# Overflow branch moved behind the expert blocks, with the expert results loaded in front of it

## The reference, cut to what matters

```python
# per token: the best of 4 groups, in it the best 2 of 8 experts, gates from two softmaxes
hid = silu(xb @ w_gate[e]) * (xb @ w_up[e])      # 1024 -> 256
y   = hid @ w_down[e]                            # 256 -> 1024
x   = x + segment_sum(y * gate, token)           # two rows for each token
x   = x + (p[i] @ w_ple[i]) * sigmoid(rmsnorm(x, g_ple[i]) @ w_ple_gate[i])
```

## Time and profile before

| | |
|---|---|
| median of 3 runs | 2473.81 us (2472.18 to 2477.26) |
| the profiled execution's own time | 2474.32 us |
| its span | 2472.4 us |
| TensorE busy | 2280.0 us, 92% |
| VectorE, ScalarE, GpSimd busy | 993.5, 588.0, 402.7 us |
| DMA | 402.86 MB, mean 163 GB/s |

### The profile page before, as it was taken

How to read it: one execution, slowest core, us unless ns; L and a number is a source line. 1 busy time by engine, 2 the same in 40 slices (tenths; PEclk the granted TensorE clock), 3 DMA queues, 4 the chain that set the end, 5 groups by cost and what they waited for, 6 DMA issues and landing times. The chain is left out here.

```text
span 2472.4 us, 29130 instructions
## 1 busy us (share of the span) xinstructions
PE 2280.0 (92%) x11792; PEld 1688.7 (68%) x11792; DVE 993.5 (40%) x1701; ACT 588.0 (24%) x1213; POOL 402.7 (16%) x399
## 2 busy tenths in 40 slices
PE   7989999689889989999698979899999999999998
PEld 6666788444447767788554446687767887888887
DVE  5545533311135444643411116455653334322234
ACT  3533301211123342410311113323441002100012
POOL 2011111112211101111111212111101211112111
PEclk9999999799989999999899999899999999999999
DMA  5114436699962202234789994332222333233321
GB/s 159 52 53 107 126 109 250 262 415 421 422 272 77 68 26 71 65 94 146 304 337 422 421 373 148 86 86 71 79 69 73 102 104 97 85 99 98 95 102 69
DMA packets 291897, 402.86 MB, mean 163 GB/s; under 512 B 31534, under 2 KB 230958, under 8 KB 273834
## 3 DMA queue, kind: packets, MB, share of 16 engines
q1 hardware_dynamic: 276000, 372.56, 42.1%
q0 software_dynamic: 10176, 16.81, 1.8%
q10 hardware_dynamic: 5578, 11.51, 1.7%
HBM read 388.98 MB, written 30.15 MB: 170 GB/s over the span
## 5 line engine op out<-in xcount | busy, mean ns | idle before, releaser
L138 PE MATMUL banks<-h_split,w_high 128*128 128x512 f32 x2624 | 825.7, 396 | 2.3 <-PEq L3142 1.7
L138 PEld LDWEIGHTS banks<-h_split,w_high 128*128 128x128 f32 x2624 | 480.9, 188 | 104.3 <-issue 8.2
L190 DVE TENSOR_TENSOR w_low<-w_raw,w_high 128x1024 fp32r<-128x1024 f32 (+1 forms) x264 | 316.8, 1201 | 502.3 <-POOL w_high L179 502.2
L179 POOL CAST w_high<-w_raw 128x1024 fp32r<-128x1024 f32 (+1 forms) x264 | 277.0, 1050 | 1458.9 <-PE banks L138 1334.1
L138 PE MATMUL banks<-h_split,w_low 128*128 128x512 f32 x1312 | 512.1, 390 | 0.0
L138 PEld LDWEIGHTS banks<-h_split,w_low 128*128 128x128 f32 x1312 | 246.2, 188 | 52.3
L138 PE MATMUL banks<-w_high,op_split 128*128 128x512 f32 x736 | 228.5, 390 | 1.4 <-DVE mg_part L1355 1.1
L1950 PE MATMUL banks<-expert_ring,ex_xsT 128*64 128x256 f32 x1472 | 181.6, 403 | 21.6 <-DMA expert_ring<-in_w_exp_up 18.6
L1950 PEld LDWEIGHTS banks<-expert_ring,ex_xsT 128*64 128x64 f32 x1472 | 108.0, 145 | 81.1 <-DMA expert_ring<-in_w_exp_up 20.5
L138 PEld LDWEIGHTS banks<-w_high,op_split 128*128 128x128 f32 x736 | 138.1, 188 | 31.9 <-DVE mg_part L1355 2.4
L138 PE MATMUL banks<-w_low,op_split 128*128 128x512 f32 x368 | 143.2, 389 | 0.0
(11 more groups left out here) (416 smaller groups left out, 2727.8 us busy)
## 6 DMA issues: line engine op xcount, KB each, us to landing
w_raw<-in_w_in SPq DMA_DIRECT2D x142, 512.0 KB, 4.0
expert_ring<-in_w_exp_gate SPq DMA_DIRECT2D x46, 1024.0 KB
expert_ring<-in_w_exp_up SPq DMA_DIRECT2D x46, 1024.0 KB
expert_ring<-in_w_exp_down SPq DMA_DIRECT2D x46, 1024.0 KB, 22.2
w_raw<-in_w_gu SPq DMA_DIRECT2D x44, 512.0 KB, 4.0
region<-in_w_exp_gate SPq DMA_DIRECT2D x20, 1024.0 KB
region<-in_w_exp_up SPq DMA_DIRECT2D x20, 1024.0 KB
region<-in_w_exp_down SPq DMA_DIRECT2D x20, 1024.0 KB, 17.6
```

What stands on the lines that cost most here:

```text
L138: last = nc.tensor.matmul(out, left, right, start=(start and n == 0), stop=(stop and n == 2), skip_group_check=True)
L179: self.nc.gpsimd.tensor_copy(self.high[:, i % self.SPLIT, 0:n], self.raw[:, i % self.RAW, 0:n]).then_inc(self.high_ready, 1)
L190: self.nc.vector.tensor_tensor(self.low[:, i % self.SPLIT, 0:n], self.raw[:, i % self.RAW, 0:n], self.high[:, i % self.SPLIT, 0:n].bitcast ...
```

## The change

The expert blocks are now part of `merge_and_route`, in the same program block as the routing. The block ends only after them, after six of the eight half-tiles of p @ w_ple, the first three splits, and after `results.load` has been issued. Then come the register load and the branch over the overflow blocks; where it is taken, it works through the 16 overflow blocks and loads the results again. The border block begins with GpSimd clearing semaphores, for which every engine waits (`swept`), and goes on with the last two half-tiles, the additions and the rest.

Within the expert blocks: TensorE starts with transposes 0, gate and up 0, hidden 0, gate and up 1, down 0, hidden 1, transposes 1, down 1, and goes on with block 2 as before. A gather's transposes are signalled in two halves, and VectorE and TensorE go on with each half. A gather is issued one pair earlier. SyncE refills the first two slots in the order gate and up 6, gate and up 7, down 6, down 7. The arithmetic for `route_spill_expert` stands behind the first pair. The space in SBUF that is kept for the descriptors of GpSimd's DMAs goes from the default of 16384 to 4096 bytes of each partition.

```diff
@@ merge_and_route
             expert_loads.issue(sp, 10)
+            for part in (e.load_gate_up, e.load_down):
+                for n in (EXPERT_SLOTS, EXPERT_SLOTS + 1):
+                    part(sp, n, n)
+            for n in range(EXPERT_SLOTS + 2, EXPERTS):
+                e.load(sp, n)
+            sp.wait_ge(spill_ready, 1)
+            for n in range(EXPERTS, e.blocks):
+                e.load(sp, n)
+            for q in (e.pairs - 2, e.pairs - 1):
+                c = (q + 1) % GATHERS
+                sp.wait_ge(e.turned, 2 * q + 2)
+                sp.dma_start(*embedding.load_pair(c)).then_inc((p_landed0, p_landed1)[c], 16)
+            sp.wait_ge(e.down_done, e.blocks - 2)
+            gate_stream.loads(sp, 0, gate_stream.RAW)
+            e.stored(sp)
+            results.load(sp)
...
+                nc.gpsimd.memset(e.xs[:, u, :], 0.0).then_inc(cleared, 1)
             pool.wait_ge(cleared, GATHERS)
             pool.wait_ge(norm.stored, 16 * NT)
             pool.wait_ge(token_ready, 2)
-            for q in range(GATHERS):
-                nc.gpsimd.indirect_dma_start(out=xs[:, q, :], out_offset=None, in_=xn_rows[:, :],
-                                             in_offset=bass.IndirectOffsetOnAxis(ap=r.token[:, q:q + 1], axis=0),
-                                             bounds_check=last_token, oob_is_err=False).then_inc(gathered[q], 16)
+            e.gather(pool, 0, last_token)
+            e.gather(pool, 1, last_token)
+            e.pooled(pool, last_token, last_row, row_ready)
+            pool.wait_ge(e.down_done, e.blocks)
+            gate_stream.split_highs(pool, 0, gate_stream.SPLIT)
...
+            pe.wait_ge(p_taken, 1)
+            e.turn(pe, 0)
+            e.gate_up(pe, 0)
+            e.turn_hidden(pe, 0)
+            e.gate_up(pe, 1)
+            e.down(pe, 0)
+            e.turn_hidden(pe, 1)
+            e.turn(pe, 1)
+            pe.wait_ge(row_ready, 1)
+            e.down(pe, 1)
+            e.multiply(pe, 2)
+            pe.wait_ge(p_landed0, 16)
+            pe.wait_ge(p_landed1, 16)
+            for i in range(EARLY_PRODUCTS):
+                wait(pe, embedding.ready, i - 1)
+                embedding.product(i, k.ps[:, i % 2, :]).then_inc(multiplied, 1)
...
+            act.preload_act_table_set("silu_and_others")
+            e.activate(act)
+            for i in range(EARLY_PRODUCTS):
+                act.wait_ge(multiplied, i + 1)
+                embedding.take(i, k.ps[:, i % 2, :])
...
+            e.weigh(dve, 0)
+            e.hidden(dve, 0)
+            e.hidden_turned(dve, 0)
+            e.hidden(dve, 1)
+            e.hidden_turned(dve, 1)
+            e.weigh(dve, 1)
+            link(V.tensor_tensor(ended, ends[:, 1:].unsqueeze(1).to_broadcast([P, SPILL, NE]),
+                                 iota[:, 0:SPILL].unsqueeze(2).to_broadcast([P, SPILL, NE]), ALU.is_le))
+            link(V.tensor_reduce(out=spill_f[:, 0:SPILL], in_=ended.bitcast(F32), axis=AX.X, op=ALU.add))
+            link(V.tensor_scalar(spill_f[:, 0:SPILL], spill_f[:, 0:SPILL], float(NE - 1), None, ALU.min),
+                 V.tensor_copy(spill_f[:, SPILL:SPILL + 1], ends[:, NE:]))
+            V.tensor_copy(r.spill_expert[:], spill_f[0:1, :]).then_inc(spill_ready, 1)
+            e.vectors(dve, 2)
+            for i in range(gate_stream.SPLIT):
+                gate_stream.split_low(dve, i)
...
-SPILL_SLOTS = (5,)
+SPILL_SLOTS = (2,)
 SBUF_END = 229344
-GATHERS = 2
+GATHERS, OUTPUTS = 2, 3
+FIRST_PAIR = 2
+EARLY_PRODUCTS = 6
...
@@ Experts
+    def load_gate_up(self, sp, n, expert):
+        U = len(self.slots)
+        wait(sp, self.gu_done, n - U + 1)
+        for dst, src in expert_parts(self.slots[n % U], *(w[self.layer, expert] for w in self.weights))[0:2]:
+            sp.dma_start(dst, src).then_inc(self.w_landed[n % U], 16)
+
+    def load_down(self, sp, n, expert):
+        U = len(self.slots)
+        wait(sp, self.down_done, n - U + 1)
+        dst, src = expert_parts(self.slots[n % U], *(w[self.layer, expert] for w in self.weights))[2]
+        sp.dma_start(dst, src).then_inc(self.down_landed[n % U], 16)
+
...
+    def gather_next(self, pool, q, last_token):
+        if q < self.pairs:
+            pool.wait_ge(self.turned, 2 * (q - GATHERS + 1))
+            self.gather(pool, q, last_token)
+
...
+    def pooled(self, pool, last_token, last_row, row_ready=None):
+        self.gather_next(pool, GATHERS, last_token)
+        if row_ready:
+            pool.wait_ge(row_ready, 1)
+        for n in range(self.blocks):
+            if n == 1:
+                self.gather_next(pool, GATHERS + 1, last_token)
+            elif n and n % 2 == 0:
+                self.gather_next(pool, n // 2 + GATHERS + 1, last_token)
+            self.scatter(pool, n, last_row)
...
+    def turn(self, pe, q):
+        pe.wait_ge(self.gathered[q % GATHERS], 16 * (q // GATHERS + 1))
+        wait(pe, self.xsT_ready, 2 * q)
+        for c in range(DC):
+            last = self.nc.tensor.transpose(self.k.ps[:, c // 4, (c % 4) * P:(c % 4 + 1) * P], self.xs[:, q % GATHERS, c::DC],
+                                            self.k.ident[:])
+            if c % 4 == 3:
+                last.then_inc(self.turned, 1)
...
+        wait(pe, self.hid_ready, n - 1)
+        for c in range(DC):
+            if c % 4 == 0:
+                pe.wait_ge(self.xsT_ready, 2 * q + 1 + c // 4)
...
+    def multiply(self, pe, start):
+        for n in range(start, self.blocks):
+            self.gate_up(pe, n)
+            if n % 2 == 0 and n // 2 + 1 < self.pairs:
+                self.turn(pe, n // 2 + 1)
+            if n > start:
+                self.down(pe, n - 1)
+            self.turn_hidden(pe, n)
+        self.down(pe, self.blocks - 1)
...
+    def weigh(self, dve, q):
+        wait(dve, self.gu_done, 2 * (q - GATHERS + 1))
+        for b in (0, 1):
+            dve.wait_ge(self.turned, 2 * q + 1 + b)
+            self.nc.vector.tensor_tensor(self.xsT[:, q % GATHERS, 4 * b:4 * b + 4, :],
+                                         self.k.ps[:, b, :].rearrange("p (c n) -> p c n", c=4),
+                                         self.r.gain[:, 4 * b:4 * b + 4].unsqueeze(2).to_broadcast([P, 4, P]),
+                                         ALU.mult).then_inc(self.xsT_ready, 1)
...
@@ spilled_experts
+    xs = k.room(ctx, tag + "_xs", [P, GATHERS, D])
...
+        for n in range(e.blocks):
+            e.load(sp, n)
+        e.stored(sp)
+        for t in range(NT):
+            sp.wait_ge(results.landed[t], 16)
+            sp.dma_start(*results.part(t)).then_inc(reloaded, 16)
+        sp.wait_ge(reloaded, 16 * NT)
...
@@ embed_per_layer
-        pe.wait_ge(embedding.ready, NT)
-        for t in range(NT):
-            embedding.product(NT + t, k.ps[:, t, :]).then_inc(multiplied, 1)
+        for i in range(EARLY_PRODUCTS, 2 * NT):
+            wait(pe, embedding.ready, i - 1)
+            embedding.product(i, k.ps[:, i % 2, :]).then_inc(multiplied, 1)
...
-        for t in range(NT):
-            act.wait_ge(multiplied, t + 1)
-            embedding.take(NT + t, k.ps[:, t, :])
+        for i in range(EARLY_PRODUCTS, 2 * NT):
+            act.wait_ge(multiplied, i - EARLY_PRODUCTS + 1)
+            embedding.take(i, k.ps[:, i % 2, :])
...
@@ border
+    done, swept = sweep
     with k.nc.Block() as block:
         @block.sync
         def _(sp):
-            moe[0](sp)
+            sp.wait_ge(swept, 1)
             ple[0](sp)
             attention[0](sp)
 
         @block.gpsimd
         def _(pool):
-            moe[1](pool)
+            clear(k, pool, done)
+            pool.sem_inc(swept, 1)
             ple[1](pool)
             attention[1](pool)
 
         @block.tensor
         def _(pe):
-            moe[2](pe)
+            pe.wait_ge(swept, 1)
             ple[2](pe)
             attention[2](pe)
...
@@ first_layer
-        ended = k.used_sems - lasting
+                                   gate_stream.low_ready, gate_stream.used, swept]}
+        merge_and_route(k, "rt", st, attention, yb_ready, m, op, r, xn_rows, route_loads, expert_loads, embedding, gate_stream,
+                        results, e, ended)
         ctx.close()
         spilled = nc.values_load(r.spill_expert[0:1, SPILL:SPILL + 1], min_val=0, max_val=SPILL)
         with nc.If(spilled > ALWAYS - EXPERTS), ExitStack() as rest, nc.Block() as block:
-            more = experts(k, rest, rest, "sp", r, i, EXPERTS, SPILL, xn_rows, y_rows, *weights, xs, gathered)
+            more = spilled_experts(k, rest, "sp", tiles, r, i, xn_rows, y_rows, weights, results)
...
@@ kernel
-    nc = bacc.Bacc("TRN2", target_bir_lowering=False, num_devices=1)
+    nc = bacc.Bacc("TRN2", target_bir_lowering=False, num_devices=1, dynamic_dma_scratch_size=4096)
```

(9 more changed lines are left out.)

338 lines of the change are left out of this document (143 added, 195 removed).

## The result

The changed kernel takes 2458.04 us (median of 4 runs, 2457.09 to 2460.14) beside 2473.64 us of the kernel before (median of 4 runs): a ratio of 0.9936, with a 95% interval of 0.9919 to 0.9953. The forecast was 2464.8, with a range from 2460.5. The direction was right; 15.6 us were gained where 9.0 were forecast. So the way is certain, and the size is known only to some 4 us.

What follows compares the result with a forecast made beforehand. The prediction took weight traffic to bound the expert blocks; terms 1 and 2 (-19.4 us) and term 3 (+10.4) gave -9.0 against the profiled 2474.32, hence a median of 2464.8 us, range 2460.5 to 2472.

Steps and rivals of the forecast that it cites:

- What bounds the stage: Expert blocks: time is the weight traffic; savings count only if refills start earlier or run with fewer holes.
- Term 1: Start of the expert blocks: block end and branch leave the path from gather to transposes; first refill 8.6 and 8.2 us earlier.
- Term 2: Expert refills: the new order of SyncE's queue closes a hole behind the first refill, 1.3 us in each layer.
- costed at nothing: Silu table load, gates, overflow arithmetic, SyncE's wait, GpSimd's queue with its gathers, and later loads: priced at 0 us.
- Term 3, the additions: Behind the experts: VectorE's additions wait for a block end after six evictions, 4.7 us later in each layer.
- Term 3, the clock: Behind the experts: TensorE's pause drops its clock, half-tiles and transposes outlast the additions; 0.5 us lost in each layer.
- A: Expert start gives less: clock rises no sooner, hole only moves; 14.0 us gained, tail costs 10.4; 2470.2 us, chance 0.13.
- B: Branch behind the experts: VectorE pays like TensorE and a microsecond more, 4.3 us a layer; 2473.4 us, chance 0.07.
- C: GpSimd's descriptors run out of room, 160 us a layer, about 2785 us; chance 0.05 together with other tail losses.

Runs made afterwards that it cites:

- the dummies: Kernel before plus seven matmuls without use in TensorE's two waits in front of the gate product: 2472.18 us, ratio 0.9999.
- the repeat: The changed kernel run once more, unchanged, in another set of runs: 2460.53 us, ratio 0.9954 to the kernel before.

## Why the prediction was wrong

**What bounds the stage: half right.** That "the time is the weight traffic" holds for the changed kernel: its gate and up matmuls wait 25.8 us for weights in the first layer and 26.2 in the second. In the kernel before it was 10.9 and 15.6, beside the 15.6 and 14.0 for gathers. That "between them the queue is never empty" was read from one stretch of 20 us in the first layer, and is wrong for the second, where 1260 to 1264 shows 266 and 346 GB/s.

**Term 1: right in sum, by parts that were off.** Forecast 16.8, measured 15.4. In the first layer the clock was full only at 465.1 (0.72 for 464 to 466), 6.2 us behind the first transpose, where 4.2 were taken, and the block's matmuls took 5.72 us instead of 4.7. In the second it rose after 4.2 us, and the term was met. By the runs, the branch with its register load is 4.4 and 3.8 us of it.

**Term 2: one of the two steps that failed.** The term has one hole, priced at 1.3 a layer, and then "between them the queue is never empty". The hole was there and the new order closed it: 1.4 and 1.3 by the stretch, 0.8 and 0.7 by the traffic. But the queue of the kernel before ran low again: 16 to 24 us behind the first refill, 0.4 and 1.1 us, and in the first layer another 1.1 us behind that, while gathers were late. All this is gone in the changed kernel, and its stretch is 2.1 and 3.6 us shorter. In the second layer some 1.2 of the 3.6 are the last 30 us of the stage, which differ as much between like kernels. The schedule's other parts stood under what is costed at nothing: the reordering of the first two blocks was counted only for the first refill, and the gathers were looked at only for the harm that they might do. How the gain is shared among them is read from the traces and not shown by a run of each.

**Term 3, the additions: right.** 5.1 in each layer where 4.7 was taken from bounds of 4.2 and 5.5. The barrier waited for ScalarE, the sixth eviction was where it was put, and the 1.8 us behind it were 2.13.

**Term 3, the clock: the other step that failed, and the larger one, 4.4 us.** Its sign was wrong. "I take 0.5 us in each layer" with 0 and 2.5 as ends: the range left out a gain. The pause of TensorE was seen, and that its half-tiles would run at half clock (5.85 us against the 6.9 forecast). The traces show the clock only as a share of full speed, 0.50 for what the prediction calls 1.2 GHz. What I did not carry on is that the product of the kernel before already paid for such a pause, 47.5 and 47.8 us where 45.7 are possible, and that the half-clock time now lies under the additions (a clock of 0.50 from about 715 to 721, additions up to 722.9). In the kernel before with the dummies this is 1.5 and 1.8 us; in the changed kernel 1.8 and 2.1. In the repeat it is 0.2 and 2.1, so the second layer's gain is in both executions and the first layer's is luck.

**The last block** (1.7 us) was not in the forecast, and the runs don't tell what decides it.

**The rivals.** A (2470.2) had 14.0 us for the start and the hole together; the start alone gave 15.4, and with the stretch it is 21.1. B: no; VectorE's branch took 0.07 us. For the low chance that the forecast gave it, the trace of before had only the 0.06 us at the old place. Why TensorE's branch takes long and VectorE's does not, no trace shows; TensorE's price is not fixed: 3.3 us at the old place in the kernel before, 5.0 and 5.4 at the new in the changed kernel. C: no; the kernel before with 4096 bytes is at 1.0003. The run shows only that nothing waits for room that the time would tell; how many transfers fit is not shown.

## What to carry to other kernels

A stage "bound by traffic" has still to be asked, for each engine that releases the traffic, what it waits for, and its traffic is to be read in 2 us stretches over the whole stage, in each layer: one stretch in the middle of one layer hid a second hole. Idle time alone does not tell the price: 14.0 us of waiting for gathers cost the second layer's traffic 0.1 us, since the queue lasted. Price a moved pause of TensorE at both of its places: where the clock was low before is a cost that can go away, and half-clock work was free here because another engine ended later (the two half-tiles at 722.6, VectorE's additions at 722.9). And the branch, moved from one path to another, had its price at both ends (10.7 us gained in front, the product 10.6 us later behind); it was the reordering that came with it which made the change worth while.

## What the runs showed that was not expected

- TensorE's branch over the body lasts 3.3 us where the DMA engines are nearly idle (a share of 0.03 and 0.05 in the kernel before) and 5.0 and 5.4 us where the results are being loaded (0.95 and 0.91 in the changed kernel). With four half-tiles in front, at 1.01 and 0.98, it lasts 6.0 and 6.7 us; with eight, at the new place too but at 0.14 and 0.38, 3.3 and 3.7 us. That the load is the reason was not tried by itself.
- Taking that branch out behind the experts gains nothing (2460.02 against 2458.04 and 2460.53 us); TensorE then pauses four times in front of the product (1.14 to 1.93 us in the first layer), whose length goes from 45.7 to 48.5 and 47.2 us.
- Adding seven useless matmuls made the product that follows 1.5 and 1.8 us shorter, at 1.4 and 1.7 us of delay.
- Three parts of a schedule that cost 1.3, 0.4 and 0.2 us of stretch when each is undone alone cost 3.8 when they are undone together, with the place of transposes 1 and of down 1.
